# A transformer kernel's expert stages: gathered rows staged in a second buffer, weight loads joined and unchained, the token table by matmuls

## What is computed

```
g_idx = top_1(softmax(h @ w_rg + b_rg))             # one of 4 groups
e_top, e_local = top_2(e_logits of that group)      # two of its 8 experts
weights = p_top * softmax(e_top)
expert(x) = (silu(x @ w_gate[e]) * (x @ w_up[e])) @ w_down[e]
out[t] = sum over the token's two experts of weight * expert(h[t])
```

## Time and profile before

| | |
|---|---|
| median of 3 runs | 3297.98 us |
| profiled execution | 3299.51 us, of which the span of instructions is 3297.7 us |
| mean granted TensorE clock | 0.875 of full |
| TensorE matmuls busy | 2522.0 us, 76% of the span |
| VectorE, ScalarE, GpSimd busy | 1129.3, 942.6, 382.1 us |
| moved by DMA | 565.87 MB, mean 172 GB/s |
| e0, first weight load to last y copy | 612 to 1209 us |
| e1 | 1849 to 2236 us |
| e2 | 2886 to 3246 us |

### The profile page before, as it was taken

One profiled execution on the slowest core, in us unless ns is written; L12 is line 12 of the kernel. 1 busy time (PEld: TensorE's weight loads), 2 busy tenths in 40 slices (PEclk: granted clock), 3 DMA queues, 4 the chain that ended last, 5 costly groups with the idle time before them and its releaser, 6 DMA issues. The chain is left out here.

```text
span 3297.7 us, 51074 instructions
## 1 busy us (share of the span) xinstructions
PE 2522.0 (76%) x17895; PEld 1944.4 (59%) x17896; DVE 1129.3 (34%) x2435; ACT 942.6 (29%) x1720; POOL 382.1 (12%) x716
## 2 busy tenths in 40 slices
PE   5974798388788758699898378884969998648882
PEld 4963698254444437576677266663847676626662
DVE  4447334210000025546543311115634753411113
ACT  2333223111112122245432123332234532213331
POOL 0000000111111110000000233331000000123332
PEclk9987899689889989799999588896979999768886
DMA  3201221599999953122121579993222121199994
GB/s 117 78 1 52 75 92 52 176 375 382 378 377 369 376 199 123 33 57 64 48 64 51 178 257 308 312 310 125 64 56 57 49 64 55 51 306 324 313 327 172
DMA packets 416210, 565.87 MB, mean 172 GB/s; under 512 B 28706, under 2 KB 303778, under 8 KB 416076
## 3 DMA queue, kind: packets, MB, share of 16 engines
q1 hardware_dynamic: 397932, 538.84, 49.0%
q0 software_dynamic: 18144, 25.24, 2.5%
HBM read 559.47 MB, written 35.97 MB: 181 GB/s over the span
## 5 line engine op out<-in xcount | busy, mean ns | idle before, releaser
L1008 PE MATMUL ps<-e_wg,e_xT 128*64 128x128 f32 (+1 forms) x2688 | 429.2, 322 | 78.5 <-issue 65.1
L1008 PEld LDWEIGHTS ps<-e_wg,e_xT 128*64 128x64 f32 x2688 | 344.7, 147 | 206.5 <-issue 158.3
L1010 PE MATMUL ps<-e_wu,e_xT 128*64 128x128 f32 (+1 forms) x2688 | 429.0, 322 | 0.0
L1149 DVE TENSOR_TENSOR e_hid<-e_silu,ps 64x128 f32<-64x128 f32 (+1 forms) x210 | 69.1, 334 | 947.6 <-ACT e_silu L1058 886.5
L1010 PEld LDWEIGHTS ps<-e_wu,e_xT 128*64 128x64 f32 x2688 | 344.3, 147 | 0.0
L1030 PE MATMUL ps<-e_wd,e_hidT 128*64 128x512 f32 x1112 | 304.1, 682 | 9.4 <-ACT e_hidT L1061 6.5
L1885 PE MATMUL ps<-t_hT,t1a_t1g_w 128*128 128x512 f32 x768 | 199.2, 411 | 4.6 <-DVE t1a_t1g_w L1907 2.4
L1885 PE MATMUL ps<-t_hT,t0a_t0g_w 128*128 128x512 f32 x768 | 199.2, 411 | 4.6 <-DVE t0a_t0g_w L1907 2.4
L447 POOL TENSOR_TENSOR all_x<-all_x,ln_rows 128x1024 f32<-128x1024 f32 x16 | 48.2, 3041 | 1261.4 <-DVE all_x L440 1261.4
L1058 ACT ACTIVATE e_silu<-ps 64x128 f32<-64x128 f32 (+1 forms) x210 | 62.3, 303 | 436.4 <-PE ps L1010 435.6
L1885 PEld LDWEIGHTS ps<-t_hT,t1a_t1g_w 128*128 128x128 f32 x768 | 145.4, 194 | 45.7 <-issue 10.3
(11 more groups left out here) (595 smaller groups left out, 4696.0 us busy)
## 6 DMA issues: line engine op xcount, KB each, us to landing
e_wd<-in_w_down SPq DMA_DIRECT2D x32, 2048.0 KB
e_wd<-in_w_exp_down SPq DMA_DIRECT2D x64, 1024.0 KB
e_wg<-in_w_exp_gate SPq DMA_DIRECT2D x54, 1024.0 KB
e_wu<-in_w_exp_up SPq DMA_DIRECT2D x54, 1024.0 KB
e_wg<-in_w_gate SPq DMA_DIRECT2D x22, 2048.0 KB
e_wu<-in_w_up SPq DMA_DIRECT2D x22, 2048.0 KB
m_h<-in_w_gate SPq DMA_DIRECT2D x10, 2048.0 KB
m_hT<-in_w_up SPq DMA_DIRECT2D x10, 2048.0 KB
```

Of the source, the lines that this page charges most:

```text
L1008: nc.tensor.matmul(ps_gu[q][0:SLOTS], xT[:, c, :], wg[s][:, c, span], start=c == 0, stop=c == DC - 1)
L1010: last = nc.tensor.matmul(ps_gu[q][SLOTS:P], xT[:, c, :], wu[s][:, c, span], start=c == 0, stop=c == DC - 1)
L1149: vec.tensor_tensor(hid[SLOTS:P, q], silu[SLOTS:P, q], ps_gu[q][SLOTS:P], ALU.mult).then_inc(hid_ready, 1)
```

## The change

The host lays out gate and up of an expert together, partition by partition, so that one partition's part of both is one run (32 KB in e0, 16 KB in e1 and e2), and down likewise (16 KB and 8 KB). One DMA loads gate and up, another down. The waits of loads on earlier loads and on the token scatters are gone; a load waits only for its buffer. TensorE waits for down only ahead of L1030's matmuls. Three loads of e0 (six of e1 and e2) are issued ahead of the others, without a wait for the token table; the ring's size is as before.

The token table is made on chip: DVE splits each slot number into block and position and compares them with two iotas, TensorE multiplies position and block indicators (16 matmuls), DVE makes the two tables. The indirect DMAs, the table in HBM and its reload are gone.

A gather lands in `landing`. DVE copies it to `gathered` when it has landed and the block before is turned (`stage_rows`), and POOL issues the next gather after this copy, three blocks ahead. The scaling of `x` in e1 and e2 is moved ahead of the first gather's staging. The diff of the core:

```diff
-    EARLY = 5 * 512 // FF
-    DEPTH = 2
+    EARLY = 3 * 512 // FF
...
+        landing = st.sb("landing", [SLOTS, D])
         gathered = st.sb("gathered", [SLOTS, D])
...
                 def load(e, s, m):
-                    w, dram = ((wg, wg_dram), (wu, wu_dram), (wd, wd_dram))[m]
-                    sp.dma_start(w[s], dram[bass.ds(e, 1)].rearrange("e p c f -> p (e c) f")).then_inc(w_sem[s][m], 16)
+                    if m == 0:
+                        sp.dma_start(wgu[s].rearrange("p m c f -> p (m c f)"),
+                                     w_gate_up[bass.ds(e, 1)].rearrange("e p m c f -> p (e m c f)")).then_inc(w_sem[s][0], 16)
+                    else:
+                        sp.dma_start(wd[s].rearrange("p c f -> p (c f)"),
+                                     w_down[bass.ds(e, 1)].rearrange("e p c f -> p (e c f)")).then_inc(w_sem[s][1], 16)
...
-                sp.wait_ge(zero_ready, 1)
-                sp.dma_start(token_dram.rearrange("(b s) one -> b (s one)", s=SLOTS), zero[:]).then_inc(zero_stored, 16)
...
-                sp.wait_ge(token_scattered, 16 * 2 * TT)
-                for q in range(2):
-                    sp.dma_start(tokrow[:, q], token_dram.rearrange("(b s) one -> b (s one)", s=SLOTS)).then_inc(tokrow_landed, 16)
                 for n in range(EARLY, len(first)):
-                    done_s, done_m = first[n - DEPTH]
-                    sp.wait_ge(w_sem[done_s][done_m], 16)
...
                     sp.wait_ge(gu_ready, end * 2)
-                    sp.wait_ge(w_sem[prev][1], landed)
                     load(e + RING, s, 0)
-                    sp.wait_ge(w_sem[prev][2], landed)
+                    sp.wait_ge(y_ready, end)
                     load(e + RING, s, 1)
-                    sp.wait_ge(y_ready, end)
-                    sp.wait_ge(w_sem[s][0], (turn_ + 2) * 16)
-                    load(e + RING, s, 2)
...
-                pe.wait_ge(tokrow_landed, 32)
-                nb = TABLE
-                nc.tensor.transpose(ps_tok, tokrow[:].rearrange("b q s -> b (q s)"), ident[0:nb, 0:nb]).then_inc(tokT_ready, 1)
+                pe.wait_ge(hot_slots_ready, 1)
+                for j in range(2):
+                    for t in range(TT):
+                        for q in range(2):
+                            last = nc.tensor.matmul(ps_tok[q * SLOTS:(q + 1) * SLOTS], at_pos[:, j, t, :], at_blk[:, j, t, :],
+                                                    start=j + t == 0, stop=j + t == TT)
+                last.then_inc(tokT_ready, 1)
...
-                    for m in range(3):
-                        pe.wait_ge(w_sem[s][m], (turn_ + 1) * 16)
+                    pe.wait_ge(w_sem[s][0], (turn_ + 1) * 16)
...
-                        pe.wait_ge(rows_gathered, (g + 2) * 16)
+                        pe.wait_ge(rows_staged, g + 2)
                         turn()
...
+                        pe.wait_ge(w_sem[s][1], (turn_ + 1) * 16)
                         pe.wait_ge(y_copied, g + 1)
...
-                vec.tensor_copy(sloti[:], slotf[:]).then_inc(table_ready, 1)
+                link(vec.tensor_scalar(blk_up[:], slotf[:], 1.0 / SLOTS, 0.5 / SLOTS - 0.5, ALU.mult, ALU.add))
+                link(vec.tensor_scalar(blk_up[:], blk_up[:], ROUND, None, ALU.add))
+                link(vec.tensor_scalar(blk[:], blk_up[:], -ROUND, None, ALU.add))
+                link(vec.scalar_tensor_tensor(pos[:], blk[:], -float(SLOTS), slotf[:], ALU.mult, ALU.add))
...
+                def stage_rows(n):
+                    dve.wait_ge(rows_gathered, (n + 1) * 16)
+                    vec.tensor_copy(gathered[:], landing[:]).then_inc(rows_staged, 1)
+
+                if alpha != 1.0:
+                    dve.wait_ge(rows_stored, 16)
+                    link(vec.tensor_scalar(x[:], x[:], alpha, None, ALU.mult))
+                stage_rows(0)
                 turn_copy(1)
+                stage_rows(1)
...
                         turn_copy(g + 2)
+                        stage_rows(g + 2)
...
-                for t in range(TT):
-                    for j in range(2):
-                        nc.gpsimd.indirect_dma_start(token_dram, bass.IndirectOffsetOnAxis(sloti[:, j, t:t + 1], 0),
-                                                     k["choice"][:, j, t:t + 1], None).then_inc(token_scattered, 16)
...
-                    nc.gpsimd.indirect_dma_start(gathered[:], None, rows_dram, bass.IndirectOffsetOnAxis(tokcur[:], 0),
+                    nc.gpsimd.indirect_dma_start(landing[:], None, rows_dram, bass.IndirectOffsetOnAxis(tokcur[:], 0),
                                                  bounds_check=S - 1, oob_is_err=False).then_inc(rows_gathered, 16)
...
-                pool.wait_ge(turned, 1)
-                gather(1)
+                for n in (1, 2):
+                    pool.wait_ge(rows_staged, n)
+                    gather(n)
...
-                        pool.wait_ge(turned, g + 2)
-                        gather(g + 2)
+                        pool.wait_ge(rows_staged, g + 3)
+                        gather(g + 3)
```

More of the change, by code:

```diff
@@ L27 @@
 MAX_BLOCKS = NE + 2 * S // SLOTS
-TABLE = MAX_BLOCKS + 2
-ROWS = TABLE * SLOTS
+TABLE = MAX_BLOCKS + 3
+ROUND = 12582912.0
 class Stage:
@@ L748, in _ @@
                 g.memset(k[n][:], 1.0)
-            for n in ("ident", "mask_le", "mask_lt", "mask_ge", "second"):
+            for n in ("ident", "mask_le", "mask_lt", "mask_ge"):
                 g.memset(k[n][:], 0.0)
+            g.memset(k["second"][:], -2.0)
             g.iota(k["iota_e"][:], [[1, NE]], 0, 0, allow_small_or_imprecise_dtypes=True)
@@ L842, in moe @@
         hidT = st.sb("hidT", [P, NF, SLOTS])
-        y = st.sb("y", [P, D // 2])
         aside = st.sb("aside", [1, 1])
-        w_sem = [[st.sem(f"{m}_landed{s}") for m in ("gate", "up", "down")] for s in range(RING)]
+        w_sem = [[st.sem(f"{m}_landed{s}") for m in ("gate_up", "down")] for s in range(RING)]
         router_landed = st.sem("router_landed")
         rows_stored = st.sem("rows_stored")
-        zero_ready = st.sem("zero_ready")
-        zero_stored = st.sem("zero_stored")
         logits_ready = st.sem("logits_ready")
@@ L866, in moe @@
         rows_gathered = st.sem("rows_gathered")
-        gathered_cleared = st.sem("gathered_cleared")
+        landing_cleared = st.sem("landing_cleared")
+        rows_staged = st.sem("rows_staged")
         turned = st.sem("turned")
@@ L1071, in _ @@
                 vec = nc.vector
-                vec.memset(zero[:], float(2 * S)).then_inc(zero_ready, 1)
-                vec.memset(gathered[:], 0.0).then_inc(gathered_cleared, 1)
+                vec.memset(landing[:], 0.0).then_inc(landing_cleared, 1)
                 link(vec.memset(gpad[:], -BIG * 1e8))
@@ new lines, in _ @@
+                dve.wait_ge(tokT_ready, 1)
+                vec.tensor_scalar(part[:, 0], ps_tok, 1.0, float(4 * S + 2), ALU.is_lt, ALU.mult)
+                vec.tensor_scalar(part[:, 1], ps_tok, float(S), float(-S), ALU.is_gt, ALU.mult)
+                link(vec.tensor_scalar(part[:, 2], ps_tok, 2.0, k["second"][:], ALU.mult, ALU.add))
+                link(vec.scalar_tensor_tensor(part[:, 3], ps_tok, -1.0, part[:, 1], ALU.add, ALU.add))
+                vec.tensor_tensor(choicecol[:], part[:, 2], part[:, 0], ALU.add).then_inc(tokcol_ready, 1)
@@ L2074, in program @@
             with Stage(nc, "m3") as s3:
-                h = s3.sb("h", [P, TT, D])
-                hT = s3.sb("hT", [P, DC, S])
+                both = s3.sb("both", [P, 2, TT * D])
+                h = both[:, 0].rearrange("p (t d) -> p t d", t=TT)
+                hT = both[:, 1].rearrange("p (c s) -> p c s", c=DC)
                 rms_rows(nc, "m3n", [(lambda t: x[:, t, :], lambda t: h[:, t, :], TT, D)], 1e-6)
@@ L2129, in rows_of, with by_partition @@
     return np.ascontiguousarray(np.concatenate([parts[n] for n in ROWS_.at]))
-_DIRECT = ["x", "mem", "w_in", "w_out", "w_q_x", "w_kv_x", "w_o_x", "w_rg", "b_rg", "w_re", "b_re", "w_gate", "w_up",
-           "w_down", "w_in_2", "mla_w_uq_2", "mla_w_ukv_2", "w_branch_2", "w_o_2", "w_router_group_2", "b_router_group_2",
-           "w_router_expert_2", "b_router_expert_2", "w_exp_gate_2", "w_exp_up_2", "w_exp_down_2"]
+_DIRECT = ["x", "mem", "w_in", "w_out", "w_q_x", "w_kv_x", "w_o_x", "w_rg", "b_rg", "w_re", "b_re",
+           "w_in_2", "mla_w_uq_2", "mla_w_ukv_2", "w_branch_2", "w_o_2", "w_router_group_2", "b_router_group_2",
+           "w_router_expert_2", "b_router_expert_2"]
+def by_partition(w):
+    layers, experts, rows, width = w.shape
+    return w.reshape(layers, experts, rows // P, P, width).transpose(0, 1, 3, 2, 4)
 def laid_out(inputs):
     arrays = {n: np.ascontiguousarray(inputs[n]) for n in _DIRECT}
+    for n in ("", "_2"):
+        stem = "w_exp_" if n else "w_"
+        arrays[f"{stem}gate_up{n}"] = np.ascontiguousarray(np.stack(
+            [by_partition(inputs[f"{stem}{m}{n}"]) for m in ("gate", "up")], axis=3))
```

(1 more changed line is left out.)

91 lines of the change are left out of this document (43 added, 48 removed).

## The result

The kernel after takes **3253.89 us** (median of 4 runs, 3251.06 to 3256.83) against 3297.26 us of the kernel before in the same set of runs. The ratio is 0.9869, with a 95% interval of 0.9852 to 0.9886: faster by 1.3%, some 43 us. The forecast was 3140 us with a range from 3080 to 3230, so the direction was right and the size wrong by more than two thirds. The profiled execution took 3251.97 us.

What follows compares the result with a forecast made beforehand. It took e0 to be bound by weight transfers, e1 and e2 by a mixture with round trips. Terms -73 (e0), -39 (e1), -46 (e2) sum to -158 against 3299.5: 3141.5, median 3140 us; range 3080 to 3230.

Steps and rivals of the forecast that it cites:

- Token table: Last slot reduction to first gather: 9.7 us instead of 20.3; net gain 9.9 us in stage e0.
- The charge of 1.5 us for scaling x beside a gather's issue: Before the first gather of stages e1 and e2: scaling moved there costs 1.5 us, 0.5 given back; net gain 8.5.
- Longer runs in e0: Weight loads of stage e0 at 420 instead of 377 GB/s; last y copy 1135 instead of 1208.5, -73 us.
- The pause while the ring is full: Start of stage e0: ring of three full near 657, first gate and up work done near 664; about 2 us.
- The tail: End of stage e0, after the loads: TensorE's backlog of 24 us becomes about 17.
- Landing 6.0 us and 8.1 us for a block that waits, in e1 and e2: Scatter and gather loops 8.1 us, 26 blocks per stage, the rest at 7.07; -39 us in e1, -46 in e2.
- third rival: Gathers and scatters queue behind long runs: landing 9.8 us, block 11.9, e1 +112, e2 +82; 3419 us, chance 0.09.
- break-even: Blocks of stages e1 and e2: total change zero at a block of 10.1 us, a landing of 8.0 us.
- The staging copy costs nothing: DVE's copy of gathered rows, before a hid product 2 us later: no cost unless the landing is late.
- second rival: Weight queue: runs are cut or the rate stays near 391 GB/s; -37 - 39 - 46, 3176 us, chance 0.20.
- 3262: Case of weight rate staying at 377 GB/s and scatter landing at 6.7 us: -17 - 2 - 17, 3262 us.
- The fit of the prediction: Weight queue: engine time is 36.4 us per MB plus 17 ns per packet; 440 GB/s without a packet cost.

Runs made afterwards that it cites:

- e1: As a run, not the stage: kernel after with every weight load in runs of 4 KB, nothing else changed; 3208.88 us, ratio to before 0.9737.
- e4: Kernel after with each weight load again waiting until the load before last has landed; 3241.14 us, ratio to before 0.9833.
- e2: As a run, not the stage: kernel after with two y buffers, taken in turn by even and odd experts; 3242.31 us, ratio to before 0.9828.
- e10: Kernel after with 4 KB runs and two y buffers taken in turn, gathers still staged; 3202.08 us, ratio to before 0.9733.
- e3: Kernel after with one gather buffer: staging copy and landing buffer removed; 3230.59 us, ratio to before 0.9807.
- e5: Kernel after with 4 KB runs and one gather buffer, no staging copy; 3220.55 us, ratio to before 0.9754.
- e11: Kernel after with 8 KB runs in stage e0, 4 KB in the other two expert stages, and two y buffers; 3191.83 us, ratio to before 0.9681.

## Why the prediction was wrong

**Token table: right.** This is the timeline of e0, which answers to the earlier trace rows:

```profile
636.16 0.61 DVE L1111 TENSOR_REDUCE e_slotf<-e_picked 128x4 f32<-128x128 f32 x2
...
642.40 0.20 DVE L1132 TENSOR_TENSOR e_tokcol<-e_part 64x51 uint32<-64x51 f32 x1
...
645.10 1.04 POOL L1188 DMA_INDIRECT e_landing<-e_dram_rows,e_tokcur  x1 [0.65 <-issue]
...
657.50 0.69 DVE L1145 COPY e_gathered<-e_landing 64x1024 f32<-64x1024 f32 x1 [14.90 <-DMA e_landing<-e_dram_rows,e_tokcur]
```

From the end of the reduction at 636.77 to the first gather are 8.3 us; forecast 9.7, before 20.3. In e1 and e2 the stretch up to the first y copy became 7.9 and 10.0 us shorter, forecast 8.5. The charge of 1.5 us for scaling x beside a gather's issue wasn't needed: it ran from 1836.19 to 1838.47, and the first gather of e1 was issued at 1839.62.

But in e0 the first gather was waited for until 657.50, 12.4 us after its issue (6.8 us in e1's run with 4 KB, 648.20 to 655.04), so that only 6.7 us of the gain reached the first y copy.

**Longer runs in e0: right mechanism, sizes off.** I had the loads end at 1116 and the last y copy at 1135; they ended near 1138 (the DMA view gives 211.93 MB for the stage, and the last slices empty there) and at 1160.45. Three terms make the 25 us, within rounding. The rate was 409 GB/s, not 420: 211.5 MB take 517 us instead of 504, **13 us**. The pause while the ring is full was to be 2 us; the first refill was issued only at 670.62, since the first gather was late, and in two slices of 13.65 us the engines moved 332 and 173 GB/s: (77 + 236) / 409 x 13.65 = 10 us, **8 us** more. The tail is 22 us instead of 17, **5 us** more.

That SP no longer waits for landings was right; it waits for buffers, as the waits of SP over 680 to 1180 us show:

```profile
SPq L895 <- PE ps L997: 239.9, 28, 19.4
SPq L898 <- PE ps L1018: 133.0, 27, 10.0
```

**Landing 6.0 us and 8.1 us for a block that waits, in e1 and e2: this step failed.** The number of such blocks was about right: 26 forecast, and 27 and 25 y copies waited for a scatter with 4 KB runs, 23 and 23 in the kernel after. The blocks that wait for none were right too, 7.07 us forecast and 6.6 to 7.2 on average. What failed is the price of a block that waits. It is 10.14 us in e1 and 10.24 in e2 in the kernel after, and 8.91 and 9.08 with 4 KB runs, where I had 8.1.

One part is the delay behind long packets. I kept the landing of the kernel before and judged that what a scatter waits behind is a quantity of bytes, which the joined loads leave as it was. In e0, with the weight queue busy throughout, the landing follows the packets: 6.2 us with 4 KB and 6.1 with the old lengths, 6.9 with 8 KB, 12.1 with 21.8 KB on average. In e1 and e2 the waits end 6.5, 7.2 and 7.98 us after the issue with 4, 8 and 10.9 KB, but 6.3 with 10.9 KB and chained loads (e4). There the unchained queue, which my sum gave no price, seems to have its part. The delay by the long packets costs 26 us in e1 (334.0 - 308.3) and 20 in e2 (295.2 - 275.6).

The other part stands with 4 KB runs as well. There I would have had 288 us for e1's blocks and 253 for e2's; the run has 308 and 276. The 27 and 25 blocks that wait, at 0.8 and 1.0 us above my price, make it up. My 6.0 us was the median over e0's scatters, while those that a copy of e1 waits for end at 6.45. The scatter loop was not left untouched either, as POOL issues the scatter behind the gather's staging: e2 and e10 took ACT's wait away, and DVE's wait and the time from y copy to scatter issue rose. How the rest divides, no run shows.

This is the place that the third rival named, with a smaller price: I had 9.8 us and 11.9 us a block for it, and its break-even at 8.0 us. With 7.98 measured the sum was still -47, since only 23 of the 37 blocks in e1 wait for the scatter; my rule for the break-even put every block in the loop. Against this rival I had set that the landing is at most 6.7 us "in all stages". The row holds e0 alone, and in e1 a y copy of the kernel before waited until 8.3 us after the issue. The rule of the Trainium skill, DMA: Bandwidth & Descriptors, section Queues, rings and completion order, which speaks of whole packets of descriptors drained before an engine switches, pointed the right way. The rows show that e0's landing behind packets five times as long on average (4 to 21.8 KB) takes twice as long, not five times.

**"The staging copy costs nothing": wrong beside long runs.** The proviso of that sentence, "unless the landing is late, and then it is the same loop", is what happened, and it cost some 20 us (e3). With 4 KB runs it costs nothing that can be measured and may give a few us (e1 against e5).

Of the 111 us missing, e0's blocks and first y copy make 25, the late landing in e1 and e2 some 45, and the blocks that I had too short even so some 43; 2 came back in the other stretches.

**The range.** Its upper end, 3230, lies above the second rival's 3176. The third rival had 0.09 and all its chance at 3419. The truth lay between the forecast and that price. The one figure near it, 3262 for a rate of 377 GB/s and a landing of 6.7 us, is near by luck: e0's rate did rise, to 409 GB/s, and the time was lost in e1 and e2. A mechanism may come at a fraction of the strength that was worked out for it.

## What to carry to other kernels

Where small latency-bound transfers (gathers and scatters that a loop waits for) share the engines with a stream, choose the stream's run length by what that stage is bound by: long runs where it is the transfers, 4 KB where it is the round trip. Here 4 KB had 400 of the 409 GB/s. A buffer added to one of two round trips of like length shows the other; measure both loops first, and test an added buffer again after the transfers beside it have changed, since the second gather buffer cost some 20 us beside long runs and nothing measurable beside short ones. Of a bundle of edits price each by itself: here the longest runs, taken alone, were worth nothing, and the rest of the change with runs of 4 KB gave 89 us.

## What the runs showed of the hardware that I had not expected

Landing against packet length in e0, where the weight queue is busy throughout: 6.2 us (4 KB), 6.9 (8 KB), 12.1 (21.8 KB on average). Between the ends that is (12.1 - 6.2) / 17.8 = 0.33 us per KB. An engine moves 25.6 KB per us there (409 / 16), so one KB is 0.039 us, and the slope is that of eight to nine packets. A scatter has 128 slots of 2 KB, eight for each of 16 engines if spread evenly. But the trace of the kernel after records it as 64 packets of two slots, four an engine, and slots without a token carry no row: 29 of the 64 carry two rows on average. So how engines divide their turns between the two queues stays open.

In e1 and e2 the same packets are late only part of the time, 17 of 36 scatters over 7 us in e1, and 4 of 38 when at most two loads are in flight (e4).

The rate hardly rises with packet length beyond 4 KB: 400, 406 (8 KB, e11) and 409 GB/s (21.8 KB mean), all with a share of 1.01 to 1.03. The fit of the prediction, with 17 ns per packet, had 440 for a packet without end, and so about 430 at 21.8 KB; it doesn't hold there. The 425 GB/s of the Trainium skill, DMA: Bandwidth & Descriptors, section Bandwidth, were not reached either in a mean over 400 us.

TensorE's granted clock moved with the waits: 0.88 of full in e1's blocks after the change, 0.93 in the fastest version, where it waits less. Its busy time per block went from 285.66 / 38 = 7.5 us to 268.05 / 38 = 7.1. A shorter wait may thus have given more than its own length; how much of e11's gain is this, no run separates.
